# Placing the row that the dots multiply by in PSUM, and the mixers' wide buffer in two banks

## What is computed

```python
h = rms_norm(x) * (1 + sc1) + sh1
proj = h @ w_in
bu_re = einsum('gph,blgh->blgp', bb_re, ug)      # the input product of the state-space group
...                                               # scan, gating, attention
x = x + g1 * (mix @ w_out)
h = rms_norm(x) * (1 + sc2) + sh2
# peer_ffn, for every token t and its 128 experts e with gates g:
act = gelu(einsum('tkd,td->tk', peer_u[e], h))   # the dots
x = x + g2 * einsum('tk,tkd->td', g * act, peer_v[e])
```

## Time and profile before

| | us |
|---|---|
| median of 3 runs | 3637.86 |
| lowest, highest | 3611.9, 3642.46 |
| span of the profiled execution | 3629.6 |
| busy: POOL, DVE, PE, ACT | 2284.8, 2225.7, 1850.4, 251.1 |

### The profile page before, as it was taken

The page is one execution under the profiler, slowest core; times in us unless marked ns, Lnnn a source line. Parts: engine busy times, 40 slices in busy tenths (PEclk is TensorE's granted clock), DMA queues, the critical chain, the costliest instruction groups (busy, mean ns, idle before and its releaser), DMA issues.

```text
span 3629.6 us, 30323 instructions
## 1 busy us (share of the span) xinstructions
PE 1850.4 (51%) x10176; PEld 903.9 (25%) x10176; DVE 2225.7 (61%) x5807; ACT 251.1 (7%) x683; POOL 2284.8 (63%) x2067
## 2 busy tenths in 40 slices
PE   6826462747364552665637455464636465332334
PEld 4425130513041230331314122231304123000000
DVE  5367757675768556864476746676485855744430
ACT  1200100001000100101000010000000010000000
POOL 0015667677677766556666766667676766777664
PEclk8767575867576776777757666676867677556557
DMA  6547899999999999999999999999999989999997
GB/s 247 202 158 271 295 409 355 368 368 389 382 368 369 338 412 376 409 397 402 389 354 375 355 354 409 337 372 368 369 372 361 360 325 408 353 371 360 384 351 293
DMA packets 314670, 1282.62 MB, mean 353 GB/s; under 512 B 34954, under 2 KB 35210, under 8 KB 303506
## 3 DMA queue, kind: packets, MB, share of 16 engines
q0 software_dynamic: 294912, 1073.87, 78.0%
q1 hardware_dynamic: 18740, 201.83, 13.7%
q10 hardware_dynamic: 864, 4.99, 0.4%
HBM read 1272.16 MB, written 8.39 MB: 353 GB/s over the span
## 4 chain that ended last, share of the span: by engine, by line
POOL 33%; PE 16%; DVE 16%; DMA 16%; issue 14%; another core or an unknown queue 5%; ACT 1%; SPq 0%; POOLq 0%; DVEq 0%; ACTq 0%
POOL ringV L245 18%; POOL ringU L226 14%; DMA ringV<-in_peer_v,idxP 7%; DMA ringU<-in_peer_u,idx_g 6%; PE py L504 5%; DVE ringU L828 5%; PE pj L576 4%; DMA ringU<-in_peer_u,idx_w 1%; PE pj L647 1%; PE pj L743 1%; PE pj L519 1%; PE pw L544 1%; POOL ringU L237 1%; PE pj L583 1%
## 5 line engine op out<-in xcount | busy, mean ns | idle before, releaser
L828 DVE CUSTOM_DVE_ANT_0 ringU<-ringU,h2g 128x1024 f32<-128x1024 f32 x1024 | 1223.1, 1225 | 811.9 <-DMA ringU<-in_peer_u,idx_g 562.5
L245 POOL DMA_INDIRECT ringV<-in_peer_v,idxP x968 | 1093.0, 1129 | 549.7 <-issue 264.1
L226 POOL DMA_INDIRECT ringU<-in_peer_u,idx_g x960 | 1070.8, 1115 | 467.7 <-issue 280.9
L504 PE MATMUL py<-ringV,wm 128*32 128x512 f32 x3968 | 799.9, 914 | 1079.7 <-DMA ringV<-in_peer_v,idxP 866.7
L504 PEld LDWEIGHTS py<-ringV,wm 128*32 128x32 f32 x3968 | 155.4, 144 | 1587.9 <-issue 1519.6
L576 PE MATMUL pj<-hT,wring 128*128 128x128 f32 (+1 forms) x2560 | 330.4, 293 | 22.0 <-issue 13.8
L576 PEld LDWEIGHTS pj<-hT,wring 128*128 128x128 f32 (+1 forms) x2560 | 317.7, 202 | 58.6 <-issue 45.2
L226 POOL DMA_INDIRECT ringU<-in_peer_u,idx_w x64 | 63.7, 996 | 274.1 <-DVE gate_w L1324 247.9
L717 PE MATMUL pw<-hT,ckv_all 128*128 128x128 f32 x320 | 79.8, 404 | 111.0 <-issue 74.6
L743 PE MATMUL pj<-wring,mixT 128*128 128x512 f32 x256 | 120.8, 632 | 7.5 <-issue 6.8
L519 PE MATMUL pj<-ident,wk 128*128 128x128 f32 x168 | 43.3, 362 | 119.9 <-DVE wk L1190 60.5
(11 more groups left out here) (298 smaller groups left out, 1951.3 us busy)
## 6 DMA issues: line engine op xcount, KB each, us to landing
wring<-in_w_in SPq DMA_DIRECT2D x28, 2048.0 KB
wring<-in_w_mod SPq DMA_DIRECT2D x24, 2048.0 KB
wring<-in_w_out SPq DMA_DIRECT2D x16, 2048.0 KB
wring<-in_peer_w_q SPq DMA_DIRECT2D x16, 2048.0 KB
ringV<-in_peer_v,idxP POOLq DMA_INDIRECT x992
ringU<-in_peer_u,idx_g POOLq DMA_INDIRECT x960
wring<-in_w_in SPq DMA_DIRECT2D x8, 784.0 KB
x_mix<-xs SPq DMA_DIRECT2D x8, 512.0 KB
```

Source lines behind the costliest of these rows:

```text
L226: pool.indirect_dma_start(out=ringU[k % NR][:, :], out_offset=None, in_=ux, in_offset=bass.IndirectOffsetOnAxis(ap=idx[:, k:k + 1], axis=0 ...
L245: pool.indirect_dma_start(out=ringV[r % NR][:, :], out_offset=None, in_=vx, in_offset=bass.IndirectOffsetOnAxis(ap=idx[:, at:at + 1], axis=0),
L504: mm = t.matmul(py[32 * j:32 * j + 32, c * 512:(c + 1) * 512], wm[e % 2][:, at:at + 32], down_row(4 * m + j)[0][:, c * 512:(c + 1) * 512], ...
L828: v.tensor_tensor_reduce(out=ringU[k % NR][:, :], in0=ringU[k % NR][:, :], in1=h2g[:, :], scale=1.0, scalar=0.0, op0=ALU.mult, op1=ALU.add ...
```

## The change

`h2p`, two banks of PSUM, takes the place of `h2g`, and the dots read it. pw has two banks. So what stood in four banks is done in two halves, or moves to pj:

- `injected(part)` computes quarters 0 and 1, then 2 and 3. Part 1 waits until DVE has used part 0, and stands behind the third weight group. DVE multiplies in two parts of 512 columns.
- index scores 2 and 3 wait for the relus of 0 and 1;
- transposed probabilities go through pj[0] alone, the sums over values through pj[1], the products with w_uv and the transposed weights through pj[0];
- modulation results use the banks of their partial sums;
- of the 16 key-score fields eight stand in pw and four in each pj.

```diff
-        h2g, g2g = sb("h2g", D), sb("g2g", D)
+        g2g = sb("g2g", D)
...
-        pw = ps("pw", 4 * 512)
+        pw = ps("pw", 2 * 512)
+        h2p = ps("h2p", D)
...
+        def key_place(f):
+            src, at = (pw, f) if f < 8 else (pj[(f - 8) // 4], f % 4)
+            return src[:, at * 128:(at + 1) * 128]
...
                         if n >= 2:
-                            t.wait_ge(S["part_sb"], n - 1)
+                            t.wait_ge(S["mod_sb"], n - 1)
...
-                    def injected():
-                        t.wait_ge(S["proj_sb"], 1)
+                    def injected(part):
+                        if part == 0:
+                            t.wait_ge(S["proj_sb"], 1)
+                        else:
+                            t.wait_ge(S["bu_used"], 1)
                         for ri, BB in enumerate((BBre, BBim)):
                             for j in range(2):
-                                for q in range(4):
+                                for i in range(2):
+                                    q = 2 * part + i
...
                     across(pj[0][:, 384:512], wt, 512, 384, 128).then_inc(S["proj_ps"], 1)
+                    if not is_first(b):
+                        injected(1)
                     mix(mix_by(b, "projected", 2))
...
+                        if h >= 2:
+                            t.wait_ge(S["relu_sb"], h - 1)
-                        t.matmul(pw[:, h * 512:h * 512 + W], pr[lo:lo + 64, at:at + 128], kiT_all[lo:lo + 64, 0:W],
+                        t.matmul(pw[:, (h % 2) * 512:(h % 2) * 512 + W], pr[lo:lo + 64, at:at + 128], kiT_all[lo:lo + 64, 0:W],
...
-                        if h >= 2:
-                            t.wait_ge(S["pt_sb"], h - 1)
+                        if u is not None and h == turnover(b) + 2:
+                            t.wait_ge(S["wT_sb"], 1)
                         for s in range(b + 1):
-                            turn(pj[h % 2][:, s * 128:(s + 1) * 128], wk[...],
+                            turn(pj[0][:, s * 128:(s + 1) * 128], wk[...],
...
-                        v.tensor_tensor_reduce(out=ringU[k % NR][:, :], in0=ringU[k % NR][:, :], in1=h2g[:, :],
+                        v.tensor_tensor_reduce(out=ringU[k % NR][:, :], in0=ringU[k % NR][:, :], in1=h2p[:, :],
...
-                    note(v.tensor_tensor(q4(t1), bre, cosq, ALU.mult))
-                    note(v.tensor_tensor(q4(t2), bim, sinq, ALU.mult))
-                    note(v.tensor_tensor(q4(t3), bim, cosq, ALU.mult))
-                    settled()
-                    v.tensor_tensor(q4(t4), bre, sinq, ALU.mult).then_inc(S["bu_used"], 1)
+                    for part in range(2):
+                        v.wait_ge(S["bu_ps"], part + 1)
+                        qs = slice(2 * part, 2 * part + 2)
+                        note(v.tensor_tensor(q4(t1)[:, qs], bre, cosq[:, qs], ALU.mult))
+                        note(v.tensor_tensor(q4(t2)[:, qs], bim, sinq[:, qs], ALU.mult))
+                        note(v.tensor_tensor(q4(t3)[:, qs], bim, cosq[:, qs], ALU.mult))
+                        settled()
+                        v.tensor_tensor(q4(t4)[:, qs], bre, sinq[:, qs], ALU.mult).then_inc(S["bu_used"], 1)
...
-                    note(v.tensor_copy(h2g[:, :], hh[:, :]))
+                    note(v.tensor_copy(h2p[:, :], hh[:, :]))
```

More of the change, by code:

```diff
@@ L344, in modulation @@
                             a.wait_ge(S["mod_ps"], n + 1)
-                            copy(modb[:, n * 512:(n + 1) * 512], pw[:, 1024 + (n % 2) * 512:1536 + (n % 2) * 512], "mod_sb")
+                            copy(modb[:, n * 512:(n + 1) * 512], pw[:, (n % 2) * 512:(n % 2 + 1) * 512], "mod_sb")
                             columns(mix_by(b, "mod", n))
@@ L414, in evac_p @@
                             a.wait_ge(S["o_ps"], h - 1)
-                        copy(hT[:, (h % 2) * 512:(h % 2) * 512 + W], pj[h % 2][:, 0:W], "pt_sb")
+                        copy(hT[:, (h % 2) * 512:(h % 2) * 512 + W], pj[0][:, 0:W], "pt_sb")
                         if h in (3, 7):
@@ L419, in evac_p @@
                                 a.wait_ge(S["mix_ready"], 2)
-                            copy(pr[:, (h // 4) * 512:(h // 4 + 1) * 512], pw[:, 1024:1536], "o_sb")
+                            copy(pr[:, (h // 4) * 512:(h // 4 + 1) * 512], pj[1][:, :], "o_sb")
                     for h in range(AH):
@@ L436, in leg @@
                     a.wait_ge(S["yc_ps"], 1)
-                    copy(mixT[:, 512:1024], pw[:, 1536:2048], "yc_sb")
+                    copy(mixT[:, 512:1024], pj[0][:, :], "yc_sb")
                     columns(mix_by(b, "values"))
@@ L608, in leg @@
                     if not is_first(b):
-                        injected()
+                        injected(0)
                     else:
@@ L633, in leg @@
                         t.wait_ge(S["bb_in"], 2)
-                        injected()
-                        t.wait_ge(S["bu_used"], 1)
+                        injected(0)
+                        injected(1)
+                        t.wait_ge(S["bu_used"], 2)
                         t.wait_ge(S["proj_sb"], 4)
@@ L730, in leg @@
                     t.wait_ge(S["o_sb"], 2)
-                    if u is not None:
-                        t.wait_ge(S["wT_sb"], 1)
                     for h in range(AH):
-                        mm = t.matmul(pw[64 * (h % 2):64 * (h % 2) + 64, 1536 + (h // 2) * 128:1664 + (h // 2) * 128],
+                        mm = t.matmul(pj[0][64 * (h % 2):64 * (h % 2) + 64, (h // 2) * 128:(h // 2 + 1) * 128],
                                       wuv[:, h * 64:(h + 1) * 64], pr[:, h * 128:(h + 1) * 128], start=True, stop=True)
@@ L757, in key_scores @@
                             for f in heads:
-                                mm = t.matmul(pw[:, (half * 8 + f) * 128:(half * 8 + f + 1) * 128],
+                                mm = t.matmul(key_place(half * 8 + f),
                                               pr[64 * half:64 * half + 64, f * 128:(f + 1) * 128],
```

34 lines of the change are left out of this document (15 added, 19 removed).

## The result

The change makes the kernel slower: 3710.9 us median of 4 runs (3697.3 to 3721.3) against 3629.6 for the kernel before beside it, ratio 1.021 (95% interval 1.018 to 1.025), where 3575 was predicted. The profiled execution has a span of 3719.5 us. First the page of the changed kernel: busy times, DMA by slice, the chain that ended last, and the groups that answer to the earlier trace rows.

The account below looks back on a forecast made before the run. No engine full; DMA fed unevenly by POOL, whose gathers the dots hold. 3629.6 - 89 + 24 + 2 = 3566.6 us of span, plus 8.3 to the median: 3575 us, range 3494 to 3655.

Parts of the forecast that it names:

- Holding and its end: POOL's gathers: dots with two SBUF operands hold them, 352 us in all; a PSUM operand ends most of it.
- Rival C: Gathers on POOL: holding is not in the second SBUF operand, they stay at 1.12 us; 3664 us, chance 0.03.
- The gain, 89 us: Gathers no longer held: 84 us over seven rounds plus 5 us for the last stretch, bounds 0 and 185.
- 20 us of a round are lost to DMA moving under 409 GB/s: Three slow DMA stretches of one round lose 3.4, 6.8 and 10.0 us against 409 GB/s.
- 12 of them come back: Slow DMA stretches: freed gathers return 12 us of the 20 a round, 84 us for seven rounds.
- The lower bound of the gain, 0: Freed gathers might give nothing, because DMA is busy anyway.
- The cost, 24 us: DVE's wait at the second half of the input product, 4 us counted per round, bounds 0 and 60.
- 10 us for DVE's longer stand: Input product: the sums start at 1084.0 instead of 1074.2, 10 us longer in each of six rounds.
- ringU and ringV have eight buffers, so 4 us per round count: Gather rings: about half the buffers are out, another eight gathers cover 10 us, so 4 us per round count.
- Rival B: Second half of the input product: the 10 us pass through six times, gain only 15; 3685 us, chance 0.09.
- the range's upper edge: Whole kernel: a gain of 20 us with half the bound of cost, 3655 us.
- The 2 us for the other halves: Index scores, modulation, attention products and the copy of hh, done in halves or moved: 2 us, bounds 0 and 10.

Follow-up runs that it names:

- e3: Kernel before, dots still reading SBUF, but py in one bank into which both halves of the columns are summed; ratio 0.999.
- e2: Kernel before with its four-bank pw, py in one bank for both column halves, and the dots reading a PSUM row; ratio 1.003.
- e1: Changed kernel with the dots reading their row from SBUF (h2g) again, the halving of pw kept; ratio 1.013.
- e6: Kernel before with the expert rows of peer_v fetched at half their width; ratio 0.993.
- e11: Kernel before with a small memset, waited for, behind each gather on POOL; ratio 1.022.
- e4: Changed kernel with the second half of the input product moved from behind the third weight group to ahead of it; ratio 1.008.
- e7: e4 with the dots' row back in SBUF; ratio 1.004.

## Why the prediction was wrong

- **Holding and its end: right.** Gathers of 948 and 964 ns (950 to 980 were given), POOL 1961 us (1960), the dot 1218 ns for 1225. Rival C is out. The reading of the earlier trace rows was too coarse: in the kernel before no gather took over 2.00 us, so none was held for more than 1.06 us, less than one dot, and of 2048 gathers some 370 lie between 1.0 and 1.95 us.
- **The gain, 89 us, was wrong: it is nothing** (from e3 to e2 +0.4%, from e1 to the changed kernel +0.8%). The step that failed is the one from "20 us of a round are lost to DMA moving under 409 GB/s" to "12 of them come back". It took slow DMA stretches as a price of slow gathers and counted what they would give back as a gain of the round. e6 shows that DMA's rate hardly matters, and the 0.3 us per us of e11 is the slope upwards only. DVE's row waits did fall, by 130 to 180 us in each pair (e2 and e3, e4 and e7), as the prediction said they would, but its waits for PE rose by as much, 137 and 151. The prediction held PE's part of the round to be fixed; it isn't: with free gathers the input product is read 6 us later and the first logits 9 us later (e2 against e3), which takes all that the rest of the round gives. Why PE's signals come late is open. The lower bound of the gain, 0, was argued from DMA and was too high by the 15 to 31 us that are lost.
- **The cost, 24 us, was too small.** Its 10 us for DVE's longer stand were near: from the first multiplication to the first sum DVE takes 12.4 us in five rounds and 14.6 in one, where it took 4.7, so 7.7 and 9.9 us more, most of it the wait of 7.3 us, as foreseen. But "ringU and ringV have eight buffers, so 4 us per round count" failed: taking 34 us of waits out gets 34 to 47 us back, 6 to 8 us a round, so no cover is seen. Why DVE's waits for rows later in the round didn't make it up wasn't tested. Rival B was the right mechanism here, and its price of 60 us the right size; its test, that rounds become no shorter than 415 us while row waits fall, is what came: the mean round is 427 us. It got 0.09, and gave 3685 because it kept 15 us of gain. (Two small slips change nothing: 1069.53 + 4 x 1.2 is 1074.3, and the range's upper edge by its own words is 3653.)
- **The 2 us for the other halves** were small but not small enough: e7 is at 1.004, 13 us (0 to 26), for all of the layout but the long wait, which takes in the short second waits of 2 us that are left.
- **The sum by measured terms:** 13 us for the layout, 34 to 47 for the wait, 15 to 31 for the row, 62 to 91, against 78 measured (2.1%). That is no separate proof: along either path, over e7 and e1 (13 + 34 + 31) or over e7 and e4 (13 + 47 + 17), the steps must add up to it. The spread says how far a term depends on what else is in the kernel, and on noise; only e2 against e3, 15 us, is a measurement apart.

## What to carry to other kernels

Time taken off an engine that leads the chain is worth something only if the others can use it: before counting it, slow that engine a little and look at both directions, since a kernel tuned around a stall can lose by adding to it and gain nothing by its removal. A wait put in the middle of the one serial sequence of a round passed through in full here, for all the idle time later in the round. And sum the idle time of the waiting engine by what it waits for: if one kind falls and another rises by the same amount, look at when in the round each result comes, which tells an engine that is early from one that is late.

## What the runs showed of the hardware

- A sum over one SBUF operand (1214 ns), a dot with one operand in PSUM (1218) and a sum over PSUM (1219) leave a gather at 0.95 to 0.97 us on average; a dot with two SBUF operands (1225) holds it, 1.11 to 1.16 us on average with rows of full width. The Trainium skill ("SBUF — State Buffer", section "Who interferes with whom") says that a VectorE instruction with at most one SBUF input does not contend with GpSimd (outside DVE's two-port modes); for the gathers' own duration the trace agrees (0.95 to 0.97 us).
- In kernels whose gathers run free beside DVE, PE's results are late in 20 to 34% of the listed reads against 7 to 19% where dots hold them, whether or not DVE reads PSUM; the signal comes late, and by what path isn't known.
- Halving the width of every peer_v row took 21% off the bytes and 0.7% off the time of the kernel before.
- A 120 ns memset behind each gather costs 79 us where gathers are held and nothing beyond noise (3 us more and 2 us less) where they are free.
